# An HGRN2 recurrence by levels: gate totals folded into query and key, two heads at a time, with projection slices between the levels

## The reference, cut to what matters

```python
forget = lb + (1.0 - lb) * jax.nn.sigmoid(f)
key = 1.0 - forget
log_f = jnp.log(forget)
query = jax.nn.silu(q)
# within a chunk, b = cumsum(log_f):
diff = b[:, :, :, None, :] - b[:, :, None, :, :]
decay = jnp.exp(jnp.where(causal, diff, -jnp.inf))
scores = jnp.einsum('bhtk,bhsk,bhtsk->bhts', qc, kc, decay)
o_intra = jnp.einsum('bhts,bhsv->bhtv', scores, vc)
k_to_end = kc * jnp.exp(b_last[:, :, None, :] - b)
new_state = jnp.exp(b_last)[..., None] * state + jnp.einsum('bhck,bhcv->bhkv', k_to_end, vc)
# then rmsnorm over the head, times silu(g), times w_out
```

## Time and profile before

| | |
|---|---|
| median of 3 runs | 2350.23 us (2349.43 to 2366.07) |
| profiled execution | span 2354.7 us, first to last instruction |
| PE busy in the span | 2210.7 us (94%) |
| DVE, ACT, POOL busy | 1097.0, 865.3, 971.3 us |
| mean granted PE clock | 0.967 |
| PE's longest single reason for waiting in the mixer | DVE scores L1008, 18.5 us |

### The profile page before, as it was taken

How to read it: one execution, slowest core, us unless ns; L and a number is a source line. 1 busy time by engine, 2 the same in 40 slices (tenths; PEclk the granted TensorE clock), 3 DMA queues, 4 the chain that set the end, 5 groups by cost and what they waited for, 6 DMA issues and landing times.

```text
span 2354.7 us, 25843 instructions
## 1 busy us (share of the span) xinstructions
PE 2210.7 (94%) x9850; PEld 1824.2 (77%) x9850; DVE 1097.0 (47%) x1382; ACT 865.3 (37%) x1055; POOL 971.3 (41%) x273
## 2 busy tenths in 40 slices
PE   7997889999999999999999999879999799999996
PEld 6876767888887777877788888668787578888875
DVE  6329966222223546555223223786567653222234
ACT  4536644223223344443323223313555342222232
POOL 3456533444443322325344444334343344444443
PEclk9999889999999999999999999989999899999998
DMA  4220102232223222113222232213222223222321
GB/s 159 90 89 19 36 19 89 89 106 90 101 101 111 72 72 72 54 54 126 89 96 100 89 107 107 90 54 107 90 89 72 74 85 107 89 102 94 107 98 54
DMA packets 30197, 203.14 MB, mean 86 GB/s; under 512 B 3252, under 2 KB 3508, under 8 KB 6200
## 3 DMA queue, kind: packets, MB, share of 16 engines
q1 hardware_dynamic: 30136, 202.29, 24.4%
HBM read 200.18 MB, written 2.10 MB: 86 GB/s over the span
## 4 chain that ended last, share of the span: by engine, by line
PE 71%; DVE 16%; issue 7%; ACT 4%; POOL 2%; DVEq 0%; ACTq 0%; POOLq 0%
PE bank L1309 70%; DVE aqk L1069 2%; DVE m_hi L1273 2%; DVE ssq L880 1%; POOL w_lo L440 1%; DVE zl L997 1%; DVE x L1198 1%; ACT L501 1%; DVE zl L996 1%; DVE x L1192 1%; DVE un L1067 0%; ACT w_hi L501 0%; DVE rot L1068 0%; ACT s_a L501 0%; DVE scores L1008 0%
## 5 line engine op out<-in xcount | busy, mean ns | idle before, releaser
L440 POOL TENSOR_TENSOR w_lo<-raw,w_hi 128x2048 fp32r<-128x2048 f32 x187 | 875.8, 4684 | 1302.5 <-ACT w_hi L501 1302.5
L1309 PE MATMUL bank<-u_hi,w_hi 128*128 128x512 f32 x1952 | 768.5, 394 | 36.2 <-DVE u_lo L868 14.8
L1309 PE MATMUL bank<-u_lo,w_hi 128*128 128x512 f32 x1952 | 765.1, 392 | 0.0
L1309 PE MATMUL bank<-u_hi,w_lo 128*128 128x512 f32 x1952 | 482.9, 397 | 0.0
L1309 PEld LDWEIGHTS bank<-u_hi,w_hi 128*128 128x128 f32 x1952 | 370.2, 190 | 118.4 <-issue 24.1
L501 ACT ACTIVATE w_hi<-raw 128x2048 fp32r<-128x2048 f32 x187 | 356.5, 1906 | 227.7 <-PE bank L1309 222.9
L1309 PEld LDWEIGHTS bank<-u_hi,w_lo 128*128 128x128 f32 x1952 | 373.7, 192 | 82.6 <-issue 4.2
L1309 PEld LDWEIGHTS bank<-u_lo,w_hi 128*128 128x128 f32 x1952 | 370.0, 190 | 76.5
L912 DVE TENSOR_TENSOR sq<-bank,rstd 128x512 f32<-128x512 f32 x66 | 45.6, 692 | 483.2 <-PE bank L1309 483.2
L501 ACT ACTIVATE sq<-sq 128x512 f32<-128x512 f32 x82 | 51.7, 630 | 543.9 <-DVE sq L912 497.1
L1309 PE MATMUL bank<-act_hi,w_hi 128*128 128x512 f32 x528 | 205.4, 389 | 0.0
(11 more groups left out here) (235 smaller groups left out, 2350.4 us busy)
## 6 DMA issues: line engine op xcount, KB each, us to landing
raw<-wall SPq DMA_DIRECT2D x187, 1024.0 KB, 4.7
h<-x_t SPq DMA_DIRECT2D x4, 512.0 KB, 7.0
out_t<-h SPq DMA_DIRECT2D x2, 512.0 KB, 2.8
out_t<-h SPq DMA_DIRECT2D x4, 256.0 KB, 3.0
lmask_f<-lmask_in SPq DMA_DIRECT2D x1, 512.0 KB
cs<-cs_in SPq DMA_DIRECT2D x1, 512.0 KB, 4.1
pf<-p_t SPq DMA_DIRECT2D x1, 512.0 KB, 3.5
amask<-amask_in SPq DMA_DIRECT2D x1, 256.0 KB
```

The costliest lines, as they stand in the source:

```text
L440: nc.gpsimd.tensor_tensor(w_lo[:, s, :], raw[:, s, :], w_hi[:, s, :].bitcast(F32), ALU.subtract).then_inc(lo_ready, 1)
L1309: return nc.tensor.matmul(out, lhsT, rhs, start=start, stop=stop, skip_group_check=True)
```

## The change

The recurrence needs no logarithm any more. The products of the forget gates over 2, 4, ..., 128 tokens are made directly, each from the one before (`decays` on POOL, seven small multiplies for a pair of heads, into `decay`). The levels now go from the diagonal and m = 1 up to m = 64. Between two levels the upper half of every block of the query `q_dec` is multiplied by the total of the lower half (`fold_queries`, DVE), and the lower half of the key by the total of the upper half (`fold_keys`, POOL); the next level multiplies the same two tiles. After the last fold they are the decayed query and the key decayed to the chunk's end, so `ends`, `differences`, the exponentials, the two DVE multiplies and the running sums go away.

The unit is a pair of heads in tiles of 1024 columns: four pairs of 8 steps, each step two levels (one for each head, banks 5 and 6). The tails of the pair before stand at steps 0 to 3 and 4 to 7 of the pair. The panels are read in another order (`MIX`): f and q of the first pair and the four i panels come first; f and q of the next pair and g of the current pair are run between the levels, three `k_step`s (of six matmuls) after each step of pairs 0 to 2, and the last g panel at one `k_step` a step in pair 3. POOL cuts `w_lo` into instructions of 512 columns (`lo_piece`) and places them between its folds. The first two output panels are cut into `out_step`s, which stand between the parts of the last two tails.

For lines left out below: `key`, `query`, `forget` tiles are rewritten for each pair in `forget_in`, `forgets`, `keys`, `query_in`, `first_decay` (the scaled bank, lb gate, 1 - forget, the scaled bank, query times forget); `gates`, `queries`, `sigmoids` are ACT's silu, silu and sigmoid over 1024 columns; DVE's `tail(hd, step)` runs `chunk_states` at step 1 and `head_out` at step 3, ACT's runs `keys_by_token` at 0, `head_squares` at 2, `root` at 3, and PE's runs `keys_by_token`, `chunk_states`, `outputs`, `mean_squares` at 0, 1, 2, 3. The last head has banks and tiles of its own.

```diff
+    f, q, i, g = PAN["f"], PAN["q"], PAN["i"], PAN["g"]
+    order = [f, q, i, i + 1, i + 2, i + 3]
+    for k in range(1, PAIRS):
+        order += [f + k, q + k, g + k - 1]
+    return order + [g + PAIRS - 1]
+MIX = mixer_order()
...
+        def span_of(l):
+            return 1 << (l - 1)
+        def decay_at(p, l):
+            m = span_of(l)
+            if m == 1:
+                return forget[:]
+            at = 2 * S - 4 * S // m
...
+        def halves_of(t, l):
+            m = span_of(l)
+            b = t.rearrange("p (n c) -> p n c", c=2 * m)
+            return b[:, :, 0:m], b[:, :, m:2 * m]
+        def ends_of(p, l):
+            t = decay_at(p, l).rearrange("p (n two) -> p n two", two=2)
+            to = [P, S // span_of(l), span_of(l)]
+            return t[:, :, 0:1].to_broadcast(to), t[:, :, 1:2].to_broadcast(to)
...
+            def lo_piece(p, a, b):
...
+                for k in range(a, b):
+                    c = slice(k * S, (k + 1) * S)
+                    ins = nc.gpsimd.tensor_tensor(w_lo[:, s, c], raw[:, s, c], w_hi[:, s, c].bitcast(F32), ALU.subtract)
+                if b == 4:
+                    ins.then_inc(lo_ready, 1)
+            def decays(p):
+                pool.wait_ge(forget_ready, p + 1)
+                if p > 1:
+                    pool.wait_ge(states_ready, 2 * p - 2)
+                for l in range(2, STEPS + 1):
+                    if l > 2:
+                        pool.wait_ge(decay_made, (STEPS - 1) * p + l - 2)
+                    t = decay_at(p, l - 1).rearrange("p (n two) -> p n two", two=2)
+                    nc.gpsimd.tensor_tensor(decay_at(p, l), t[:, :, 0], t[:, :, 1], ALU.mult).then_inc(decay_made, 1)
+            def fold_keys(p, l):
+                pool.wait_ge(lev_done, 2 * STEPS * p + 2 * l + 2)
+                if l > 1:
+                    pool.wait_ge(decay_made, (STEPS - 1) * p + l - 1)
+                low = halves_of(key[p % 2], l)[0]
+                nc.gpsimd.tensor_tensor(low, low, ends_of(p, l)[1], ALU.mult).then_inc(kend_ready, 1)
...
-            lo_panels(PAN["hgrn_out"] + 2, PAN["end"])
+            lo_piece(0, 0, 4)
+            lo_piece(1, 0, 4)
+            lo_piece(2, 0, 4)
+            decays(0)
+            for n in range(3, 6):
+                lo_piece(n, 0, 4)
+            for p in range(PAIRS):
+                lo_piece(6 + 3 * p, 0, 4) if p == 0 else lo_piece(6 + 3 * p, 2, 4)
+                lo_piece(7 + 3 * p, 0, 2)
+                fold_keys(p, 1)
+                lo_piece(7 + 3 * p, 2, 4)
+                fold_keys(p, 2)
+                if p < PAIRS - 1:
+                    fold_keys(p, 3)
+                    lo_piece(8 + 3 * p, 0, 2)
+                    fold_keys(p, 4)
+                    lo_piece(8 + 3 * p, 2, 4)
+                    fold_keys(p, 5)
+                    decays(p + 1)
+                    fold_keys(p, 6)
+                    lo_piece(9 + 3 * p, 0, 2)
+                    fold_keys(p, 7)
+                else:
+                    for l in range(3, STEPS):
+                        fold_keys(p, l)
+            lo_panels(HOUT + 1, PAN["end"])
...
+            for p in range(PAIRS):
+                if p:
+                    conv(7 + 3 * p)
+                for l in range(STEPS):
+                    if p:
+                        tail(2 * p - 2 + l // 4, l % 4)
+                        if l == 0:
+                            gates(p - 1)
+                    if p < PAIRS - 1 and l == 2:
+                        conv(8 + 3 * p)
+                        sigmoids(p + 1)
+                    if p < PAIRS - 1 and l == 5:
+                        conv(9 + 3 * p)
+                        queries(p + 1)
+            conv(HOUT + 1)
+            keys_by_token(HG - 2)
             keys_by_token(HG - 1)
+            gates(PAIRS - 1)
+            head_squares(HG - 2)
             head_squares(HG - 1)
+            root(HG - 2)
             root(HG - 1)
             residual(PAN["hgrn_out"], 1, 1)
             ffn(0, 1)
...
+            def both_scaled(n, t, ready, before):
+                for c in range(2):
+                    ins = tt(t[:, c * S:(c + 1) * S], pair(n)[c][:], rstd[:], ALU.mult)
+                ins.then_inc(ready, 1)
+                dve.wait_ge(ready, before + 1)
+                dve.sem_inc(group_free, 1)
+            def forget_in(p):
+                dve.wait_ge(panel_done, at_f(p) + 1)
+                if p:
...
+                    dve.wait_ge(decay_made, (STEPS - 1) * (p - 1) + 1)
+                both_scaled(at_f(p), forget, fin_ready, p)
...
+                    dve.wait_ge(ket_done, 2 * p - 2)
+                ts(key[p % 2][:], forget[:], -1.0, 1.0, ALU.mult, ALU.add).then_inc(key_ready, 1)
...
+            def first_decay(p):
...
+                tt(q_dec[p % 2][:], query[:], forget[:], ALU.mult).then_inc(qdec_ready, 1)
+            def fold_queries(p, l):
...
+                    dve.wait_ge(decay_made, (STEPS - 1) * p + l - 1)
+                high = halves_of(q_dec[p % 2], l)[1]
+                tt(high, high, ends_of(p, l)[0], ALU.mult).then_inc(qdec_ready, 1)
...
+            def take_level(p, l, a):
+                n = 2 * STEPS * p + 2 * l + a
                 dve.wait_ge(lev_done, n + 1)
...
+                bank = PB[5 + a][:].rearrange("p (n c) -> p n c", c=P)
...
+                    ins = tt(s3, bank, ident[:].rearrange("p (n c) -> p n c", n=1).to_broadcast([P, TT, P]), ALU.mult)
                 else:
...
-                    ins = nc.vector.copy_predicated(s3, lmask[:, l:l + 1, :].to_broadcast([P, TT, P]), bank)
+                    k = LEVELS.index(span_of(l))
...
+                    ins = nc.vector.copy_predicated(s3, lmask[:, k:k + 1, :].to_broadcast([P, TT, P]), bank)
...
             def head_out(hd):
                 dve.wait_ge(orstd_ready, hd + 1)
-                stt(un[:, 0, :], HB[:], vec(V_HG, 0), rstd2[:], ALU.mult, ALU.mult).then_inc(on_ready, 1)
+                stt(un[:, 0, :], tail_bank(hd)[:], vec(V_HG, 0), root_of(hd)[:], ALU.mult, ALU.mult).then_inc(on_ready, 1)
...
+            keys(0)
+            query_in(0)
+            first_decay(0)
             dve.wait_ge(masks_ready, 1)
-            decayed(0, range(RING))
-            for hd in range(HG):
-                if hd:
...
-                    decayed(hd + 1, range(RING))
+            for p in range(PAIRS):
+                for l in range(STEPS):
+                    if p and l == 0:
+                        gate_in(p - 1)
+                    take_level(p, l, 0)
+                    take_level(p, l, 1)
+                    if l:
+                        fold_queries(p, l)
+                    if p:
+                        tail(2 * p - 2 + l // 4, l % 4)
+                    if p < PAIRS - 1:
+                        if l == 2:
+                            forget_in(p + 1)
+                        elif l == 3:
+                            forgets(p + 1)
+                        elif l == 5:
+                            keys(p + 1)
+                            query_in(p + 1)
+                        elif l == 7:
+                            first_decay(p + 1)
+            gate_in(PAIRS - 1)
+            chunk_states(HG - 2)
             chunk_states(HG - 1)
+            head_out(HG - 2)
             head_out(HG - 1)
...
+            def k_step(n, k, x_hi, x_lo):
+                w = [t[:, n % 2, :].rearrange("p (k c) -> p k c", c=HALF) for t in (w_hi, w_lo)]
+                if k == 0:
+                    pe.wait_ge(lo_ready, n + 1)
+                    pe.wait_ge(group_free, n + 1)
+                for c in range(2):
+                    for a, (v, x) in enumerate(((w[0], x_hi), (w[0], x_lo), (w[1], x_hi))):
+                        ins = mm(pair(n)[c][:], v[:, k, c * P:(c + 1) * P], x[:, k, :], k == 0 and a == 0,
+                                 k == KC - 1 and a == 2)
+                if k == KC - 1:
+                    ins.then_inc(panel_done, 1)
+            def out_step(n, k):
+                pe.wait_ge(oh_ready, k + 1)
+                k_step(n, k, o_hi, o_lo)
+            def level(p, l, a):
+                n = 2 * STEPS * p + 2 * l + a
+                q = query if l == 0 else q_dec[p % 2]
+                if a == 0 and l == 0:
+                    pe.wait_ge(query_ready, p + 1)
+                    pe.wait_ge(key_ready, p + 1)
+                elif a == 0:
+                    pe.wait_ge(qdec_ready, STEPS * p + l)
+                    if l > 1:
+                        pe.wait_ge(kend_ready, (STEPS - 1) * p + l - 1)
                 if n >= 2:
                     pe.wait_ge(lev_free, n - 1)
-                a, b = (level_tile(hd, l),) * 2 if l < len(LEVELS) else (key[:, hd, :], query[:, hd, :])
-                for c in range(TT):
-                    ins = mm(near(PB[5 + l % 2], c), near(a, c), near(b, c))
+                for c in range(TT * a, TT * a + TT):
+                    ins = mm(near(PB[5 + a], c - TT * a), near(key[p % 2], c), near(q, c))
```

(38 more changed lines are left out.)

343 lines of the change are left out of this document (149 added, 194 removed).

## The result

The changed kernel takes 2381.62 us (median of 8 runs, 2374.97 to 2386.61), the kernel before beside it on the same chip 2361.04 (8 runs, 2349.43 to 2369.46). The ratio is **1.0093**, interval 1.0066 to 1.0121: slower by 0.9%, where 2327 was forecast and 2345 was the upper end of the range. The profiled execution has a span of 2378.6, 23.9 more than before.

What follows compares the result with a forecast made beforehand. PE's waits and low clock, 53.3 us from first level to output projection's end, were taken as the most to win. Five remaining loss terms sum to 30, leaving 23.3: 2350.2 - 23.3 = 2327 us, range 2308 to 2345.

Steps and rivals of the forecast that it cites:

- Need of PE: First level to output projection's end: PE needs 162.3 us of 215.6; moved panels, 76.2 us of work, cancel.
- the changes between levels and slices: Recurrence: PE switching between fp32 levels and panel slices, 32 steps at 0.2 us, 6 us lost (3 to 8).
- Step 3 in pairs 1 and 2: `head_out` waits for `root` ahead of the next `take_level` on DVE, delaying PE: 3 us with contention (0 to 10).
- step 3 in pair 3: Last pair, one `k_step` a step: `head_out` delays level 4's take and fold, so PE waits 3.5 us.
- First step of pair 3: DVE arrives late from `head_out`, `first_decay` and `gate_in`, so PE waits 1.7 us.
- The end: Last tails and output panels: PE waits for roots, second keys and states, `head_out` and `conv`, 11 us (6 to 18).
- Clock: Pair 3 and the end: short waits lower PE's granted clock over 8 us of work, costing 4 us (0 to 9).
- low clock: Rival, chance 0.20: 63 us of PE work in pair 3 and the end at clock 0.8, giving 2339 us.
- Folds: Between levels: each `fold_queries` on DVE takes 0.7 to 1.9 us, each `fold_keys` on POOL 1.15 us.
- DVE does not get in between POOL's pieces: Rival, chance 0.07: `fold_queries` and `head_out` wait behind POOL, 51 us together, giving 2378 us, slower.
- The slices do not fill: Rival, chance 0.05: late `w_lo` makes 9 panels wait, 2.6 us each, so no change at 2350 us.
- The waits are smaller: Rival, chance 0.20: the loss terms come at their low ends, 12 us, for a gain of 41, 2309 us.

Runs made afterwards that it cites:

- with the place restored: Changed kernel plus an unused 64-byte tile ahead of the activation regions, putting them back at their old addresses: 2340.25 us, ratio 0.9941 to the kernel before.
- the improved kernel: Changed kernel with the 64-byte tile, most of `head_out` after the next take and fold, `forgets` a step later, third output panel's `conv` earlier: 2328.81 us, ratio 0.9883.
- The kernel with `w_lo` whole: Changed kernel with the 64-byte tile, each `w_lo` of the recurrence in one POOL instruction of 2048 columns again: median 2350.93 us, ratio 0.9968 to the kernel before.
- an eighth: Changed kernel with 64 bytes between regions `u` and `act`, so only `act` returns to its old place: 2364.93 us, ratio 1.0071 to the kernel before.
- the change with 128 bytes more: Changed kernel with an unused 128-byte tile ahead of the activation regions, `u_hi` at byte 106432: 2351.4 us in one run.
- the kernel with the weights shifted: Changed kernel with an unused 64-byte tile ahead of the weights, `w_hi` at 49344 and `u_hi` at its old 106368: 2376.95 us in one run.

## Why the prediction was wrong

**The step that failed** is the sentence "Everything after the mixer is untouched, so I price only the stretch from the first level to the end of the output projection". The instructions are untouched, their operands' places are not. The change removes `b_last` and `e_last`; I counted them among DVE's copies and gave the tiles themselves no line. The shift of everything behind them is what cost: the 46.6 us lost behind the mixer go back to 8.1 with the place restored, and 36 to 41 us of the time return. That such a term exists no row of before shows; but the diff showed that every tile behind them moves, and it could have been listed as an unknown of 2000 us of PE's work, bounded by nothing. No rival held it: "slower" was held to need 24 us lost inside the mixer.

**The mixer, step by step**, held in its sum, partly by luck: the 22.7 us of the changed kernel hold 4.5 us of slower panels that the forecast of 23.3 did not have, and a clock that came out at 1.00 in pairs 1 and 2; with the place restored the mixer gains 21.0. One trace of each stands behind these numbers.

- Need of PE. From 88.89 to 359.78 are 270.9 us; by my rows PE needs 162.3 + 76.2 = 238.5 there, which leaves 32.4. Of that 14 panels x 0.32 = 4.5 is the slower pace. The remaining 28 stands against my 30 for five terms: 18 are the waits below, 10 are left for the changes between levels and slices and the clock together (6 and 4 forecast).
- Step 3 in pairs 1 and 2 (3 forecast) and step 3 in pair 3 (3.5): the waits for `q_dec` are 6.4 in three, at 172 and in the two lines below, where `fold_queries` is the last to end (1.98 and 2.44). The sum is right, 6.4 for 6.5; pairs 1 and 2 have 1.0 more than forecast and pair 3 has 1.1 less. The step of the working that was mis-sized there is `forgets`, put at 1.1 and measured at 2.93 beside POOL's pieces.
- First step of pair 3 (1.7): 0.97 for `scores`. Its other steps (0.2 to 0.3 each): one wait of 0.42. Somewhat less.
- The end (11): 2.2 for the root (the fifth line of the first timeline), 0.64 for the second keys, 1.2 for the second states, 4.4 in two for `o_lo`, 2.0 for `w_hi`: 10.4. Forecast 2.2, 0.6, 1.2, 4.3 and 2.6.
- Clock (4): pairs 1 and 2 have 1.00, pair 3 and the end 0.96 and 0.95. With the place restored the same program got 0.97 in pairs 1 and 2. So the clock there is not decided by the order of the work alone. The rival "low clock" was put on pair 3 and the end at 0.8; it did not happen.

The waits of pair 2 and pair 3 and of the end, after, in the timeline of PE:

```profile
229.67 2.05 PE L1439 MATMUL bank<-q_dec,key 128*128 128x128 f32 x16 [1.98 <-DVE q_dec L1102]
...
255.48 2.02 PE L1439 MATMUL bank<-q_dec,key 128*128 128x128 f32 x16 [0.97 <-DVE scores L1117]
...
275.32 2.59 PE L1439 MATMUL bank<-q_dec,key 128*128 128x128 f32 x16 [2.44 <-DVE q_dec L1102]
...
299.81 0.94 PE L1439 MATMUL bank<-val,decay 128*128 128x128 f32 x6 [0.64 <-ACT decay L580]
```

- Folds (0.7 to 1.9 on DVE; 1.15 on POOL), `decays` of a pair (3) and a piece of `w_lo` (1.17), in the groups of after from the first level to the end of pair 3:

```profile
L511 POOL TENSOR_TENSOR w_lo<-raw,w_hi 128x512 fp32r<-128x512 f32 x40 | 59.6, 1508 | 13.8 <-ACT w_hi L580 13.8
...
L532 POOL TENSOR_TENSOR key<-key,decay 128x512 f32<-128x512 f32 x24 | 27.1, 1129 | 70.9 <-PE bank L1439 70.6
...
L1102 DVE TENSOR_TENSOR q_dec<-q_dec,decay 128x512 f32<-128x512 f32 x24 | 25.0, 1043 | 0.0
```

A fold takes 1.04 on DVE and 1.13 on POOL. The pieces take 1.51, a third more than a quarter of the whole: four pieces are 6.0 against 4.69, hidden in POOL's slack.

**The rivals.** "DVE does not get in between POOL's pieces" was the only one that ended slower; it did not happen (folds of 1.04, no `q_dec` wait but at step 3), and the slowdown is not its. "The slices do not fill" did not happen either: pairs 0 to 2 have no wait for `w_lo`. "The waits are smaller" did not hold in the change, but the improved kernel made part of it true by a new order.

**And with the place restored** the forecast would still have been too high: 11.7 us of medians, an interval of 9 to 19, against 23.3. In the trace the mixer gains 383.60 - 362.65 = 21.0 (its last residual), the span 12.9. The first feed-forward block gives 2.9 back, with waits of 2.6 and 4.3 us at its start where the kernel before has one of 3.6: the price of the boundary was in no term of the forecast. The attention stage gives 7.5 back: windows before, and with the place restored.

```profile
747.40:1110.60 363.20, 339.90 (x1519) 286.09 (x1519) 201.04 (x228) 151.40 (x269) 120.49 (x26) 0.96 0.22 78
```
```profile
729.30:1100.00 370.70, 347.06 (x1519) 289.62 (x1519) 201.02 (x228) 151.59 (x269) 120.53 (x26) 0.94 0.22 76
```

Same instructions, same sums of the other engines, a clock of 0.94 instead of 0.96. The kernel with `w_lo` whole, of the same code and layout there, took 363.3. In the seven kernels at 227 ns this stage has one of two lengths in the profiled execution: 363.1, 363.3, 363.9 and 364.5, or 370.5, 370.6 and 370.7, and the kernel before with `w_lo` in pieces, whose attention is that of the kernel before, is among the long ones. So these 7 us do not belong to the change; that they explain the gap between the medians too is argued, not shown.

## What to carry to other kernels

A change that adds or removes a tile moves all that lie behind it: compare the addresses of the big operands before and after, and list a shift as a cost of its own. When a profile comes back slower, look first at a stream that the change did not touch, and compare the distance of two equal places in it: 11.20 for 10.88 says in two rows that waits alone cannot be the cause. Cutting a long POOL instruction that DVE waits behind did not help where PE stood idle between levels anyway (ratio 1.000); it helped where DVE was late already, since there 5.23 us for two passes became 2.94.

## What the runs showed of the hardware

- The pace of fp32r matmuls of 128x512 follows the distance in a partition from the loaded to the streamed operand: 227 ns where it is a multiple of 256 bytes (odd and even multiples, in seven kernels and in `act` of an eighth), 229 or 233 with 64 left, 232 to 233 with 32, 128 or 192 left. Over the kernel this is up to 2.3% (2407.39 against 2351.92). Why is open: a clash of the reads of weight load and stream fits it, and no run looked at it by itself.
- With 64 left one kernel can have both paces: 229 and 233 ns in the attention output of the change with 128 bytes more, and in the `i` panels of the kernel with the weights shifted. In both the pace changed over a break in the stream. What picks it is open.
- DVE's two passes over `forget` (one tensor operand and two columns) took 5.23 us beside a POOL instruction of 5.00, 2.94 beside two of 1.6, and 1.00 in the improved kernel, where they come later.
- One run of the kernel with `w_lo` whole took 12446.11 us, among nine of 2346 to 2353. The median of 2350.93 counts it; that of the other nine is 2350.79. The ratio goes without it, and its cause is unknown.
